# Summing half of the gathered expert rows on TensorE, through diagonals of their weights

## What is computed

```python
eidx = jnp.take_along_axis(cidx, pos, axis=-1)
g = jax.nn.softmax(top, axis=-1)
u = u_tab[eidx]
v = v_tab[eidx]
a = jax.nn.gelu(jnp.einsum('thkd,td->thk', u, xb).astype(F32))
return jnp.einsum('thk,thkd->td', (g * a).astype(v.dtype), v)
```

## Time and profile before

| | us |
|---|---|
| median of three runs | 2883.98 |
| lowest, highest | 2883.62, 2892.7 |
| span of the profiled execution | 2896.9 |

### The profile page before, as it was taken

One profiled execution on the slowest core, in us unless ns is written; L12 is line 12 of the kernel. 1 busy time (PEld: TensorE's weight loads), 2 busy tenths in 40 slices (PEclk: granted clock), 3 DMA queues, 4 the chain that ended last, 5 costly groups with the idle time before them and its releaser, 6 DMA issues.

```text
span 2896.9 us, 19315 instructions
## 1 busy us (share of the span) xinstructions
PE 1325.8 (46%) x5913; PEld 1008.8 (35%) x5913; DVE 1865.8 (64%) x2673; ACT 216.5 (7%) x539; POOL 1475.1 (51%) x989
## 2 busy tenths in 40 slices
PE   8999998778899999999500000000000000000000
PEld 7886776545587862888400000000000000000000
DVE  4105556476111041135999998999988888888887
ACT  1001111133100010020000000000000000000000
POOL 2005666360200000001487668668688888888885
PEclk9999998778899999999755555555555555555555
DMA  8434322231334448436698889889898989999997
GB/s 326 145 107 167 112 96 114 87 93 59 116 138 148 151 162 324 152 131 260 256 416 359 367 344 389 343 332 376 321 392 355 377 358 376 380 384 394 355 391 311
DMA packets 107284, 757.87 MB, mean 262 GB/s; under 512 B 12952, under 2 KB 12984, under 8 KB 17800
## 3 DMA queue, kind: packets, MB, share of 16 engines
q0 software_dynamic: 82720, 582.35, 50.9%
q1 hardware_dynamic: 24496, 174.66, 16.7%
HBM read 748.67 MB, written 12.48 MB: 263 GB/s over the span
## 4 chain that ended last, share of the span: by engine, by line
PE 40%; DVE 23%; POOL 16%; issue 11%; DMA 8%; ACT 1%; DVEq 0%; POOLq 0%; SPq 0%; ACTq 0%
PE bank L335 14%; DVE sb_mv_n L1933 9%; POOL sb_ring L1864 6%; PE bank L324 5%; POOL sb_m_t L1864 4%; PE bank L670 4%; PE bank L663 4%; POOL sb_mk_t L1864 4%; DMA sb_mk_t<-in_peer_u,sb_z_t 2%; PE bank L1357 2%; DVE sb_ring L1924 2%; DMA sb_ring<-in_peer_v,sb_z_t 2%; DMA sb_ring<-in_peer_u,sb_z_t 1%; DVE sb_m_t L1924 1%; POOL sb_z_t L1883 1%
## 5 line engine op out<-in xcount | busy, mean ns | idle before, releaser
L1864 POOL DMA_INDIRECT sb_ring<-in_peer_v,sb_z_t x132 | 285.6, 2164 | 100.2 <-DVE sb_mv_n L1933 44.7
L1933 DVE SCALAR_TENSOR_TENSOR sb_mv_n<-sb_ring,sb_h_t,sb_mv_n 128x2048 f32<-128x2048 f32 x128 | 301.6, 2356 | 51.6 <-DMA sb_ring<-in_peer_v,sb_z_t 36.9
L1864 POOL DMA_INDIRECT sb_ring<-in_peer_u,sb_z_t x124 | 264.2, 2131 | 118.7 <-DVE sb_ring L1924 66.8
L1924 DVE SCALAR_TENSOR_TENSOR sb_ring<-sb_ring,sb_y_t 128x2048 f32<-128x2048 f32 x120 | 271.4, 2291 | 37.2 <-DMA sb_ring<-in_peer_u,sb_z_t 35.6
L1825 PE MATMUL bank<-sb_h_t,sb_con 8*128 8x128 f32 x2 | 0.8, 482 | 599.8 <-DVE sb_h_t L1801 599.8
L335 PE MATMUL bank<-sb_x_t,sb_ring 128*128 128x264 f32 x1024 | 228.2, 387 | 0.0
L1870 POOL COPY sb_z_t<-sb_z_t 128x8 int32<-128x8 int32 x6 | 4.7, 788 | 429.4 <-DVE sb_z_t L1793 427.4
L1825 PEld LDWEIGHTS bank<-sb_h_t,sb_con 8*128 8x128 f32 x2 | 0.5, 305 | 600.1 <-issue 600.1
L335 PEld LDWEIGHTS bank<-sb_x_t,sb_ring 128*128 128x128 f32 x1024 | 195.1, 191 | 32.7
L1864 POOL DMA_INDIRECT sb_m_t<-in_peer_u,sb_z_t x70 | 147.4, 2106 | 55.1 <-DVE sb_m_t L1916 35.0
L335 PE MATMUL bank<-sb_y_t,sb_ring 128*128 128x264 f32 x768 | 171.2, 387 | 0.0
(11 more groups left out here) (414 smaller groups left out, 2915.7 us busy)
## 6 DMA issues: line engine op xcount, KB each, us to landing
sb_ring<-in_w_z SPq DMA_DIRECT2D x28, 1024.0 KB, 4.8
sb_ring<-in_w_xk SPq DMA_DIRECT2D x16, 1024.0 KB, 4.8
sb_ring<-in_w_xv SPq DMA_DIRECT2D x16, 1024.0 KB, 5.2
sb_ring<-in_w_out SPq DMA_DIRECT2D x16, 1024.0 KB, 4.7
sb_ring<-in_w_xq SPq DMA_DIRECT2D x16, 1024.0 KB, 4.7
sb_ring<-in_mem_k SPq DMA_DIRECT2D x16, 1024.0 KB, 4.8
sb_ring<-in_mem_v SPq DMA_DIRECT2D x16, 1024.0 KB, 6.4
sb_ring<-in_w_xo SPq DMA_DIRECT2D x16, 1024.0 KB, 4.8
```

What stands on the lines that cost most here:

```text
L1864: pool.indirect_dma_start(SLOT[slot], None, A[table], bass.IndirectOffsetOnAxis(IXS[half][:, k:k + 1], 0))\
L1924: dve.scalar_tensor_tensor(out=SLOT[k], in0=SLOT[k], scalar=1.0, in1=XN[blk], op0=ALU.mult, op1=ALU.mult, accum_out=ACTV[:, bass.ds(i * NS ...
L1933: dve.scalar_tensor_tensor(out=HN[blk], in0=SLOT[k], scalar=WGT[blk][:, bass.ds(i * NSLOT + k, 1)], in1=HN[blk], op0=ALU.mult, op1=ALU.add ...
```

## The change

Slots 1, 3, 5 and 7 of the gathered `v` rows are summed by TensorE, slots 0, 2, 4 and 6 by DVE as before. For each of TensorE's slots ScalarE makes a 128x128 diagonal of that slot's weights (the identity, scaled per partition), and TensorE multiplies the diagonal with the slot in four matmuls of 512 columns, accumulating in PSUM banks 4 to 7 over the 16 rounds of a block. After the last round DVE adds the four banks to the row (`dve_gather_sums`). The counter `peer_used` is replaced by eight, `used0` to `used7`, one for each slot; POOL keeps a register for each. Some steps move: the small matmuls of the samples go to banks 0 and 1 (and 0 to 3), `act_keys(2)` stands ahead of `act_gelu(0)`, its softmax behind ten rounds of diagonals, the samples' top-k pieces behind rounds 3, 6 and 9 of block 0's sums, `dve_samples_experts` behind round 12, and `dve_final(0)` behind the samples' sums.

```diff
+        ON_DVE, ON_PE = (0, 2, 4, 6), (1, 3, 5, 7)
+        DIAG = [x_t[:, 4096 + j * P:4096 + (j + 1) * P] for j in range(len(ON_PE))]
+
+        def emptied(g, k):
+
+            return (g - EARLY) // NSLOT + (EARLY // 4 if k >= 4 else 0)
...
                             for k in range(NSLOT):
-                                pool.wait_ge(S("peer_used"), use)
-                                pool.reg_add(use, use, 1)
+                                pool.wait_ge(S(f"used{k}"), uses[k])
+                                pool.reg_add(uses[k], uses[k], 1)
                                 gather(table, half, k, k)
...
         def dve_sums(dve, blk, lo, hi):
 
             with dve.Fori(lo, hi) as i:
-                for k in range(NSLOT):
+                for n, k in enumerate(ON_DVE):
+                    before = ON_DVE[n - 1]
                     dve.wait_ge(S(f"slot{k}"), i * 16 + landed(V_OF[blk], k))
-                    dve.wait_ge(S("peer_used"), i * NSLOT + (V_OF[blk] + k))
+                    dve.wait_ge(S(f"used{before}"), i + (emptied(V_OF[blk], before) + (n > 0)))
                     dve.scalar_tensor_tensor(out=HN[blk], in0=SLOT[k], scalar=WGT[blk][:, bass.ds(i * NSLOT + k, 1)],
-                                             in1=HN[blk], op0=ALU.mult, op1=ALU.add).then_inc(S("peer_used"), 1)
+                                             in1=HN[blk], op0=ALU.mult, op1=ALU.add).then_inc(S(f"used{k}"), 1)
+
+        def act_diagonals(act, blk, lo, hi):
+
+            if lo == 0:
+                act.wait_ge(S("wgt"), ORDER[blk] + 1)
+            base = emptied(V_OF[blk], ON_PE[0])
+            assert all(emptied(V_OF[blk], k) >= base for k in ON_PE)
+            with act.Fori(lo, hi) as i:
+                for j, k in enumerate(ON_PE):
+                    act.wait_ge(S(f"used{k}"), i + emptied(V_OF[blk], k))
+                    act.activation(DIAG[j], ident, ACT.Copy, scale=WGT[blk][:, bass.ds(i * NSLOT + k, 1)])\
+                        .then_inc(S("diag"), 1)
+
+        def pe_sums(pe, blk, lo, hi):
...
+            def one(i):
+                for j, k in enumerate(ON_PE):
+                    pe.wait_ge(S(f"slot{k}"), i * 16 + landed(V_OF[blk], k))
+                    pe.wait_ge(S("diag"), i * len(ON_PE) + (blk * rounds * len(ON_PE) + j + 1))
+                    peeled = isinstance(i, int)
+                    for q in range(4):
+                        mm = pe.matmul(bank[4 + q][:, :], lhsT=DIAG[j], rhs=SLOT[k][:, q * 512:(q + 1) * 512],
+                                       start=peeled and i == 0 and j == 0,
+                                       stop=peeled and i == rounds - 1 and j == len(ON_PE) - 1, skip_group_check=True)
+                    mm.then_inc(S(f"used{k}"), 1)
...
+        def dve_gather_sums(dve, blk):
+
+            for k in NSLOT - 1, ON_DVE[-1]:
+                dve.wait_ge(S(f"used{k}"), emptied(V_OF[blk] + SLOTS, k))
+            for q in range(4):
+                h = HN[blk][:, q * 512:(q + 1) * 512]
+                dve.tensor_tensor(h, h, bank[4 + q][:, :], ALU.add).then_inc(S("sum_acc"), 1)
...
             pe_keys(pe, 2)
+            pe_sums(pe, 0, 0, 11)
             pe_samples_experts(pe)
+            pe_sums(pe, 0, 11, 16)
             pe_samples_sums(pe)
+            pe_sums(pe, 1, 0, 16)
...
             act_keys(act, 1)
+            act_keys(act, 2)
             act_gelu(act, 0)
-            act_keys(act, 2)
+            act_diagonals(act, 0, 0, 10)
+            act_softmax(act, PARTS + 1)
+            act_diagonals(act, 0, 10, 16)
+            act_gelu(act, 2)
             act_final(act, 0)
-            act_gelu(act, 2)
             act_final(act, 2)
             act_gelu(act, 1)
+            act_diagonals(act, 1, 0, 16)
             act_final(act, 1)
...
-            dve_sums(dve, 0, 0, 4)
+            dve_sums(dve, 0, 0, 3)
             dve_keys(dve, PARTS + 1)
-            dve_sums(dve, 0, 4, 8)
+            dve_sums(dve, 0, 3, 6)
             dve_candidates(dve, PARTS + 1)
-            dve_sums(dve, 0, 8, 12)
+            dve_sums(dve, 0, 6, 9)
             dve_experts(dve, PARTS + 1)
+            dve_sums(dve, 0, 9, 12)
             dve_samples_experts(dve)
             dve_sums(dve, 0, 12, 16)
             dve_samples_dots(dve)
-            dve_final(dve, 0)
+            dve_gather_sums(dve, 0)
             dve_gelu(dve, 2)
             dve_samples_sums(dve)
+            dve_final(dve, 0)
             dve_dots(dve, 1, 0, 8)
             dve_final(dve, 2)
             dve_dots(dve, 1, 8, 16)
             dve_gelu(dve, 1)
             dve_sums(dve, 1, 0, 16)
+            dve_gather_sums(dve, 1)
             dve_final(dve, 1)
```

More of the change, by code:

```diff
@@ L1822, in pe_samples_experts @@
         def pe_samples_experts(pe):
-            pe.wait_ge(S("ex_act"), 4)
+            pe.wait_ge(S("sco_act"), PARTS + 8)
             pe.wait_ge(S("tk"), THIRD + marks(PH)[3] - 1)
-            pe.matmul(bank[4][:, 0:P], lhsT=cc("sel", rows=TS), rhs=IA[0:TS, :], start=True, stop=True)
-            pe.matmul(bank[5][:, 0:P], lhsT=cc("sel", rows=TS), rhs=WGT[2][0:TS, :], start=True, stop=True)\
+            pe.matmul(bank[0][:, 0:P], lhsT=cc("sel", rows=TS), rhs=IA[0:TS, :], start=True, stop=True)
+            pe.matmul(bank[1][:, 0:P], lhsT=cc("sel", rows=TS), rhs=WGT[2][0:TS, :], start=True, stop=True)\
                 .then_inc(S("ex_pe"), 1)
@@ L1851, in build @@
         EARLY = 2 * NSLOT
+        ON_DVE, ON_PE = (0, 2, 4, 6), (1, 3, 5, 7)
+        DIAG = [x_t[:, 4096 + j * P:4096 + (j + 1) * P] for j in range(len(ON_PE))]
+        def emptied(g, k):
+            return (g - EARLY) // NSLOT + (EARLY // 4 if k >= 4 else 0)
         def landed(g, k):
-            return 16 * ((g - EARLY) // NSLOT + 1) + (16 * EARLY // 4 if k >= 4 else 0)
+            return 16 * (emptied(g, k) + 1)
         def pool_peer(pool):
-            with pool.register("round") as rnd, pool.register("use") as use:
+            with ExitStack() as regs:
+                rnd = regs.enter_context(pool.register("round"))
+                uses = [regs.enter_context(pool.register(f"uses{k}")) for k in range(NSLOT)]
                 pool.reg_mov(rnd, 1 + 4)
-                pool.reg_mov(use, 1 + 3 * NSLOT)
+                for k in range(NSLOT):
+                    pool.reg_mov(uses[k], emptied(2 * EARLY, k))
                 def gather(table, half, k, slot):
@@ L1872, in single @@
                     for k in range(NSLOT):
[L1873 to L1877, removed]
+                        if early:
+                            slot = 4 + k % 4
+                            if g + k >= 4:
+                                pool.wait_ge(S(f"used{slot}"), (g + k) // 4)
+                        else:
+                            slot = k
+                            if emptied(g, k):
+                                pool.wait_ge(S(f"used{slot}"), emptied(g, k))
+                        gather(table, half, k, slot)
                 def gathers(table, blk, i0=0):
@@ L1906, in pool_peer @@
                 pool.reg_add(rnd, rnd, 2)
-                pool.reg_add(use, use, 2 * NSLOT)
+                for k in range(NSLOT):
+                    pool.reg_add(uses[k], uses[k], 2)
                 pool.wait_ge(S("tk"), SECOND + marks(PH)[2])
@@ new lines, in pe_sums @@
+        def pe_sums(pe, blk, lo, hi):
+            rounds = SLOTS // NSLOT
+            if lo == 0:
+                if blk == 0:
+                    pe.wait_ge(S("ex_act"), 4)
+                else:
+                    pe.wait_ge(S("sum_acc"), 4)
+            def one(i):
[8 more added lines that the diff above has]
+                    mm.then_inc(S(f"used{k}"), 1)
+            first, last = lo + (lo == 0), hi - (hi == rounds)
+            if lo == 0:
+                one(0)
+            with pe.Fori(first, last) as i:
+                one(i)
+            if hi == rounds:
+                one(rounds - 1)
@@ L1965, in act_gelu @@
             a, done = (AS, V_S) if blk == 2 else (ACTV, V_OF[blk])
-            act.wait_ge(S("peer_used"), done)
+            for k in range(NSLOT):
+                act.wait_ge(S(f"used{k}"), emptied(done, k))
             act.activation(a, a, ACT.Gelu_apprx_tanh).then_inc(S("gelu"), 1)
```

25 lines of the change are left out of this document (13 added, 12 removed).

## The result

| | before | after |
|---|---|---|
| median of four runs, us | 2883.93 | 2794.64 |
| lowest, highest | 2883.62, 2892.7 | 2791.22, 2800.64 |
| span of the profiled execution | 2896.9 | 2790.9 |

The time is 0.9686 of the one before (ratio of the means, 95% interval 0.9665 to 0.9706). The two spans are therefore 106 us apart, and 17 of these are no gain. In the later series of runs the unchanged kernel took 2888.9 to 2891.7 us in the median instead of 2883.9, so kernels of different series are compared by their ratios and not by their microseconds.

The account below looks back on a forecast made before the run. POOL, held up by DVE's instructions, was taken to pace block 1's sums, and DVE block 0's. Savings of 40 us in block 0 and 27 in block 1, less 3, took 64 off 2884.0: 2820 us, range 2798 to 2862.

Parts of the forecast that it names:

- the rivals: TensorE only just keeps up (chance 0.15), TensorE is slower than DVE was (0.08), POOL keeps its pace (0.07).
- DMA's rate: In both blocks' sums, a gather was taken to cost 2.50 us, between 2.46 and 2.53 seen in the trace.
- D1 is not touched: 0: Block 1's dots, 357 us before the sums, were expected to gain nothing.
- on DVE either way: Block 0's row scale, moved behind the samples' sums, was said to take DVE 2.4 us in either place.
- The cold start: Early in each stage of sums TensorE starts cold, first round 27 us at worst; 3 us taken off the gain.
- The clock was expected to alternate: In the sums TensorE's clock would switch between 0.50 and 1.00, free of cost if its mean exceeds 0.69.
- A slot is held: In the sums, TensorE would hold each slot 4 to 8 us instead of 3.4, with the queue staying filled.
- The ends: Bank additions and TensorE's last slot after the sums: 5 us charged in block 1, 2 in block 0.
- V0's dry time: In block 0's sums, DMA runs dry at three blocks of samples' work, 6.5 us each, 20 in all.
- Nine instructions, one per DVE instruction: In block 1's sums, each of POOL's nine instructions per round waits out one DVE instruction: 22.5 us a round.
- The rival that POOL keeps its pace: Gathers' 2.17 us are not DVE's doing, the round stays 22.5 us, total 2890 to 2895; chance 0.07.
- The diagonals, the semaphores, the moved steps: ScalarE's diagonals (1.2 us of a 20 us round), one semaphore per slot and reordered steps were each expected to cost nothing.

Follow-up runs that it names:

- e8: Changed kernel, but TensorE waits for two slots and takes them in one burst; 2799.56 us, 0.9700 of the kernel before.
- e2: Changed kernel with TensorE's four slots in block 1 only, VectorE summing all of block 0; 0.9845 of the kernel before.
- e4: Changed kernel with TensorE summing two slots of eight instead of four, in both blocks; 2805.15 us, 0.9711 of the kernel before.
- e7: Changed kernel with gathers written out and POOL's index copies gone; 2769.0 us, 0.9584 of the kernel before.
- e9: Kernel before with only `dve_final(0)` moved behind the samples' sums; 2875.64 us against 2891.65, ratio 0.9956.
- e6: Kernel before with gathers written out and POOL's index copies gone, all sums on DVE; 2821.50 us, 0.9772 of the kernel before.
- e1: Changed kernel with all eight slots summed by DVE again, semaphores and moved steps kept; 2882.57 us against 2889.86, ratio 0.9973.
- e3: Changed kernel with TensorE's four slots in block 0 only, VectorE summing all of block 1; 0.9793 of the kernel before.
- e11: The unchanged kernel before, profiled a second time in a single run; span 2886.6 us.

## Why the prediction was right and where it was off

The measured time lies outside the stated range, but the mechanism in the two stages of sums was the forecast one: DVE half relieved, POOL released from it, DMA the bound in both stages of sums, three dry places left in V0. None of the rivals came. What failed is one step taken at nothing (D1), and what was off is one size (DMA's rate). The forecast was 64 us, the measurement is 89, and the low end of the range was missed by 3.4 us. With either of the two put right, the measurement would have been inside.

**DMA's rate.** Taken as 2.50 us per gather. Where nothing is in the way it is 427 to 429 GB/s, 2.44 to 2.46 us, in S of the kernel after and in the 5-us stretch of e8, and 422 and 423 GB/s (2.48 us) over the 305 to 312 us of V1 in e2, e4 and e7. At 2.456 that is 0.044 x 256 = 11 us over both stages. In V1 of the kernel after, the 128 slots are summed and the banks added in 316.6 us, where 325 were forecast. The prediction's own row of 427 GB/s had it, and the midpoint with the 414 of another stretch was the mis-sized term.

**"D1 is not touched: 0", and the row scale "on DVE either way".** This step failed. Its instructions are not touched, but their neighbour is. The moved row scale alone is worth some 13 us (e9: 0.0044 of 2890, with an interval of 7 to 19), and D1 goes from 351.6 or 357.9 to 335.5. The trace of before had the sign of it: a gather instruction of 15.53 us at 2180, where the mean is 2.3, and a D1 of 357 us at 369 GB/s beside the 427 over 50 us of the same stage. The prediction read D1's stretch as a whole and did not ask what held POOL there. This term and the rate are most of the 25 us. What D1 still lacked after that was the index copy: without it, e7's D1 is 316.5.

**The cold start: 3 us.** V1 has a clock of 0.99 over its length and V0 0.95: no cost that can be seen. The clock was expected to alternate, and it did not; see below. A slot is held 3.7 us, not 4 to 8.

**The ends.** In V1 four additions in 2.48 us and a last slot of 3.70 us stand where one sum of 2.35 us stood: 3.8 us, where 5 were taken. In V0 2 were taken; S came out 0.7 to 1.8 us shorter.

**V0's dry time: 20 us.** V0 is 336.4 us; 128 x 2.456 is 314.4, which leaves 22 for three dry places of about 6 us each and what is round them. This term was right.

**POOL.** "Nine instructions, one per DVE instruction" held up well beyond what the prediction needed it for: e6 takes the ninth away, with all sums left on DVE, and V1 goes from 355.1 to 323.0. Its mean gather in the kernel after is 1.10 us in V1 (the forecast was under 1.6), 1.33 in V0. The rival that POOL keeps its pace had a rule behind it. The Trainium skill (SBUF — State Buffer, Who interferes with whom) says that a two-input DVE instruction holds up only such POOL instructions as read SBUF, and infers that making a DMA's descriptors needs only the write side. Here gathers go from 2.17 to about 1 us when half of DVE's two-input instructions go, and e1 to e3 turn it on and off by block. This gather reads its indices from SBUF, so the first half of the rule may well apply; the inference does not hold for it.

**The diagonals, the semaphores, the moved steps.** ScalarE is busy 25 of 316 us in V1, and every wait of TensorE shown above is for a transfer. The semaphores had no effect that can be told from the moved row scale (e1 0.9973, e9 0.9956, with intervals that overlap). The rest was taken at nothing, and nothing in e1 speaks against it, though its V1 of 361.6 us is 6.5 longer than that of before, with nearly the same busy times; e3's, 357.6, lies between. But e1's trace is its slowest run, and even two traces of kernels with the old counter and the same V1 differ by 3 us there (e11 355.1, e9 352.0). Whether the semaphores cost a little in a stage that is in lockstep is open.

**By terms**, from the forecast's 64: + 11 for the rate, + 13 for the moved scaling, + 3 for the cold start, + 1 for V1's end, + 3 in S (the 2 charged to V0's end and about 1 that S is shorter), - 2 for the dry places: 93, where 89 were measured and the spans of e11 and of the kernel after differ by 96. The traces allow no closer account, since D1 alone differs by 6 us between two traces of the same kernel.

## What to carry to other kernels

When two engines run in lockstep, count instructions and not their time: the ninth POOL instruction of a round, a copy that takes 0.20 us by itself, cost 2.0 us of each round in V1 of the kernel before, and removing it was worth 2.3% alone, where moving half the sums to another engine was worth 3.1%. A stage that falls short of a rate shown elsewhere in the same trace should be asked why, also when the change does not touch it, since a moved neighbour can undo or bring about the loss. And a share can be given out by stage: where DVE has other work to do, more slots for the helper are right, and where it has not, they make the helper the bound.
